# The routing of a mixture-of-experts layer with x turned unscaled, gathered parts made on VectorE by halves, and two sigmoids

## The reference

```
h = h + hgrn2_mixer(...)                      # the residual before
t = rms_norm_2(h, moe_norm).reshape(256, D)   # h * rsqrt(mean(h*h) + eps) * gain
logits = (t @ w_router).astype(F32)           # 256 x 8
top_vals, top_idx = lax.top_k(logits, 2)
top_w = jax.nn.softmax(top_vals, axis=-1)     # two weights per token
gates = jnp.sum(jax.nn.one_hot(top_idx, 8) * top_w[..., None], axis=1)
for e in range(8):
    out = out + gates[:, e:e + 1] * swiglu(t, w_gate[e], w_up[e], w_down[e])
```

## Time and profile before

| what | value |
|---|---|
| median of 3 runs | 1944.0 us (1942.25 to 1947.37) |
| the profiled execution, its own time | 1941.3 us |
| span of its records | 1939.4 us |
| busy in the span | PE 96%, DVE 80%, ACT 65%, POOL 1% |
| mean granted clock of TensorE | 0.981 of 2.4 GHz |

### The profile page before, as it was taken

The page is one execution under the profiler, slowest core; times in us unless marked ns, Lnnn a source line. Parts: engine busy times, 40 slices in busy tenths (PEclk is TensorE's granted clock), DMA queues, the critical chain, the costliest instruction groups (busy, mean ns, idle before and its releaser), DMA issues.

```text
span 1939.4 us, 27547 instructions
## 1 busy us (share of the span) xinstructions
PE 1854.3 (96%) x10240; PEld 1580.6 (82%) x10240; DVE 1552.2 (80%) x1589; ACT 1255.3 (65%) x1290; POOL 11.3 (1%) x9
## 2 busy tenths in 40 slices
PE   7888999998899999998799999999999999999997
PEld 7777999877799988876688888888888888888886
DVE  8966788476567645665898998989989899899997
ACT  6966565356554435554577777777777777777775
POOL 0000000000000000001000000000000000000000
PEclk9999999999799999999899999999999999999999
DMA  9422455542145554332499998999989989899894
GB/s 366 146 88 91 170 180 190 192 153 92 64 159 189 176 193 152 131 130 98 172 368 356 343 376 335 373 361 344 381 325 367 381 336 371 337 367 380 327 368 194
DMA packets 68330, 490.85 MB, mean 253 GB/s; under 512 B 7713, under 2 KB 8097, under 8 KB 8993
## 3 DMA queue, kind: packets, MB, share of 16 engines
q1 hardware_dynamic: 67968, 488.52, 67.1%
q0 software_dynamic: 288, 1.31, 0.2%
HBM read 488.75 MB, written 1.05 MB: 253 GB/s over the span
## 4 chain that ended last, share of the span: by engine, by line
PE 87%; DVE 6%; ACT 5%; issue 2%; DMA 0%; SPq 0%; ACTq 0%; DVEq 0%
PE ps L421 26%; PE ps L423 20%; PE ps L430 20%; PE ps L432 6%; PE ps L425 6%; DVE wl L2087 1%; PE ps L441 1%; PE ps L1322 1%; ACT wh L1401 1%; PE ps L1234 1%; PE ps L1053 1%; PE ps L467 1%; PE ps L1090 1%; PE ps L826 1%; PE ps L827 1%
## 5 line engine op out<-in xcount | busy, mean ns | idle before, releaser
L2990 DVE TENSOR_TENSOR wl<-raw,wh 128x2048 fp32r<-128x2048 f32 x336 | 761.1, 2288 | 63.3 <-ACT wh L2011 59.8
L2011 ACT ACTIVATE wh<-raw 128x2048 fp32r<-128x2048 f32 x336 | 642.1, 1918 | 180.9 <-PE ps L430 180.8
L421 PE MATMUL ps<-wh,hTh 128*128 128x512 f32 (+2 forms) x1128 | 443.2, 394 | 7.1 <-DVE hTl L2375 1.7
L2087 DVE TENSOR_TENSOR wl<-raw,wh 128x2048 fp32r<-128x2048 f32 x125 | 286.0, 2290 | 128.5 <-ACT wh L1401 127.9
L423 PE MATMUL ps<-wh,hTh 128*128 128x512 f32 x896 | 349.3, 390 | 0.0
L1401 ACT ACTIVATE wh<-raw 128x2048 fp32r<-128x2048 f32 x125 | 238.6, 1913 | 140.9 <-PE ps L430 73.2
L430 PE MATMUL ps<-wl,hTh 128*128 128x512 f32 (+2 forms) x1128 | 301.1, 386 | 0.0
L423 PE MATMUL ps<-wh,hTl 128*128 128x512 f32 (+2 forms) x680 | 260.4, 385 | 0.0
L421 PEld LDWEIGHTS ps<-wh,hTh 128*128 128x128 f32 x1128 | 212.2, 188 | 50.1 <-issue 5.4
L430 PEld LDWEIGHTS ps<-wl,hTh 128*128 128x128 f32 x1128 | 210.1, 188 | 42.8
L421 PE MATMUL ps<-hTh,wh 128*128 128x256 f32 x896 | 223.2, 286 | 2.5 <-DVE hTl L2127 2.3
(11 more groups left out here) (433 smaller groups left out, 2026.4 us busy)
## 6 DMA issues: line engine op xcount, KB each, us to landing
raw<-in_units SPq DMA_DIRECT2D x461, 1024.0 KB, 6.9
x<-in_x SPq DMA_DIRECT2D x2, 512.0 KB, 5.4
work<-in_lru_w SPq DMA_DIRECT2D x1, 1024.0 KB, 15.4
xn<-in_mem SPq DMA_DIRECT2D x1, 1024.0 KB, 17.5
out<-x SPq DMA_DIRECT2D x2, 512.0 KB, 3.4
consts<-in_consts POOLq DMA_DIRECT2D x1, 768.0 KB, 4.6
work<-in_moe_gain POOLq DMA_DIRECT2D x1, 512.0 KB, 3.8
consts<-in_consts SPq DMA_DIRECT2D x1, 352.0 KB, 11.5
```

Source lines behind the costliest of these rows:

```text
L421: nc.tensor.matmul(out, sh, mh, start=(first and j == 0), stop=False)
L2011: A(wh[:, n % SPLIT, :], raw[:, n % RAW, :], ACT.Copy).then_inc(sem("hi_made"), 1)
L2087: V.tensor_tensor(wl[:, n % SPLIT, :], raw[:, n % RAW, :], wh[:, n % SPLIT, :].bitcast(F32), ALU.subtract).then_inc(sem("lo_made"), 1)
L2990: V.tensor_tensor(wl[:, n % SPLIT, :], raw[:, n % RAW, :], wh[:, n % SPLIT, :].bitcast(F32), ALU.subtract).then_inc(sem("lo_made"), 1)
```

## The change

- `moe_norm_2` joins `SCALED_LATER`: TensorE turns x unscaled, into banks 4 to 7. The squares of token tile 0 are summed before ScalarE's `norm_high`, those of tile 1 behind it.
- The router's three products stand together for each k. The token's 1/std (`token_scale`) is applied when VectorE copies the turned logits to `L`.
- GpSimd computes nothing here. VectorE makes `tokens` from x, `token_scale` and the gain with `tokens_half`, and both differences with `tokens_rest`; everything about `parts` goes by halves of columns (512 of 1024, both token tiles). The first half of the gather waits for 4 steps, the second for 6 (`TOKEN_STEPS`).
- The gain is loaded into `xn` once the recurrent layer's output has been turned, not into `work` after the residual.
- The two weights are sigmoid(v1-v2) and sigmoid(v2-v1), both on ScalarE, in place of an exponential on ScalarE and three small operations on VectorE.
- VectorE makes the low part of expert unit 1 between the first and the second add of the residual, and that of unit 2, with the four memsets, behind `tokens_low`.

```diff
-    moe_gain = area(4096, D)
+    moe_gain = xn[:, 0, :]
...
+    TOKEN_STEPS = (4, 6)
...
-    NORM_BANK = {n: 4 if n in ("hgrn_norm_2", "ffn_norm_2") else 0 for n in NORMS}
-    SCALED_LATER = ("mem_attn_norm", "attn_norm_2", "ffn_norm_2")
+    NORM_BANK = {n: 4 if n in ("hgrn_norm_2", "ffn_norm_2", "moe_norm_2") else 0 for n in NORMS}
+    SCALED_LATER = ("mem_attn_norm", "attn_norm_2", "ffn_norm_2", "moe_norm_2")
...
@@ TensorE
-        split_product(ps[0:NE, 7, 0:S], [(rh[:, k * NE:(k + 1) * NE], rl[:, k * NE:(k + 1) * NE], hTh[:, k, :], hTl[:, k, :])
-                                         for k in range(KD)], ready=tile_ready, rest=lambda: None).then_inc(sem("logits"), 1)
+        for k in range(KD):
+            w = slice(k * NE, (k + 1) * NE)
+            tile_ready(k)
+            nc.tensor.matmul(ps[0:NE, 0, 0:S], rh[:, w], hTh[:, k, :], start=(k == 0), stop=False)
+            nc.tensor.matmul(ps[0:NE, 0, 0:S], rl[:, w], hTh[:, k, :], start=False, stop=False)
+            ins = nc.tensor.matmul(ps[0:NE, 0, 0:S], rh[:, w], hTl[:, k, :], start=False, stop=(k == KD - 1))
+        ins.then_inc(sem("logits"), 1)
...
-                pe.wait_ge(sem("tokens_left"), 3)
+                pe.wait_ge(sem("tokens_left"), TOKEN_STEPS[q])
...
@@ ScalarE
-        norm("moe_norm_2", N_FIXED + SPLIT)
-        for i in range(2):
-            act.wait_ge(sem("tokens_left"), i + 1)
-            A(parts[i][:], tokens[:], ACT.Copy).then_inc(sem("tokens_part"), 1)
+        A(warm, ones[:, 0:1], ACT.Sqrt)
+        norm_stats("moe_norm_2", (0,), False)
+        norm_high("moe_norm_2", 0)
+        norm_stats("moe_norm_2", (1,))
+
+        def token_part(i, h, left):
+
+            act.wait_ge(sem("tokens_left"), left)
+            cs = slice(h * HALF, (h + 1) * HALF)
+            A(parts[i][:, :, cs], tokens[:, :, cs], ACT.Copy).then_inc(sem("tokens_part"), 1)
+
+        token_part(0, 0, 1)
+        hi_to(N_FIXED + SPLIT)
+        token_part(1, 0, 2)
+        token_part(0, 1, 3)
+        token_part(1, 1, 5)
+        act.wait_ge(*reached("route_diff", 1))
+        A(rtv["w1"], rtv["v2"], ACT.Sigmoid, scale=-1.0)
+        A(rtv["w2"], rtv["v2"], ACT.Sigmoid).then_inc(sem("route_exp"), 1)
...
-        act.wait_ge(*reached("route_diff", 1))
-        A(rtv["ex"], rtv["v2"], ACT.Exp).then_inc(sem("route_exp"), 1)
...
@@ GpSimd
-        pool.wait_ge(*reached("x_ready", X_AFTER["hgrn"]))
+        pool.wait_ge(*reached("hgrn_oT_ps", 4))
         pool.dma_start(moe_gain, moe_gain_d.partition_broadcast(P)).then_inc(sem("moe_gain"), 16)
-        pool.wait_ge(*reached("norm_xn", TT * len(NORMS)))
-        pool.wait_ge(sem("moe_gain"), 16)
-        for t in range(TT):
-            ins = G_.tensor_tensor(tokens[:, t, :], xn[:, t, :], moe_gain, ALU.mult)
-        ins.then_inc(sem("tokens_left"), 1)
-        pool.wait_ge(sem("tokens_part"), 1)
-        pool.wait_ge(sem("tokens_left"), 1)
-        G_.tensor_tensor(tokens[:], tokens[:], parts[0][:], ALU.subtract).then_inc(sem("tokens_left"), 1)
...
@@ VectorE
-        residual("hgrn_x_change", 7, N_FIXED, 0)
+        residual("hgrn_x_change", 7, N_FIXED, 0, N_FIXED + 2)
...
-        norm("moe_norm_2", N_FIXED + SPLIT - 1)
+        norm_low("moe_norm_2", 0)
+        norm_rows("moe_norm_2")
+        token_scale = rstd[:, 2 * NORM_OF["moe_norm_2"]:2 * NORM_OF["moe_norm_2"] + TT]
...
+        def tokens_half(t, h):
+            cs = slice(h * HALF, (h + 1) * HALF)
+            return V.scalar_tensor_tensor(out=tokens[:, t, cs], in0=x[:, t, cs], scalar=token_scale[:, t:t + 1], in1=moe_gain[:, cs],
+                                          op0=ALU.mult, op1=ALU.mult)
+
+        def tokens_rest(i, h, part):
+
+            dve.wait_ge(sem("tokens_part"), part)
+            cs = slice(h * HALF, (h + 1) * HALF)
+            V.tensor_tensor((tokens, parts[2])[i][:, :, cs], tokens[:, :, cs], parts[i][:, :, cs],
+                            ALU.subtract).then_inc(sem("tokens_left"), 1)
...
-        V.tensor_copy(logitsT, ps[0:NE, 7, 0:S]).then_inc(sem("logits_read"), 1)
+        V.tensor_copy(logitsT, ps[0:NE, 0, 0:S]).then_inc(sem("logits_read"), 1)
+        tokens_half(0, 0)
+        tokens_half(1, 0).then_inc(sem("tokens_left"), 1)
...
-        lo_to(N_FIXED + SPLIT)
+        tokens_rest(0, 0, 1)
+        tokens_half(0, 1)
+        tokens_half(1, 1).then_inc(sem("tokens_left"), 1)
```

More of the change, by code:

```diff
@@ L314, in rows_of @@
     def rows_of(name):
-        return area(0, TT, D) if name == "mem_attn_norm" else xn
+        return {"mem_attn_norm": area(0, TT, D), "moe_norm_2": area(10240, TT, D)}.get(name, xn)
     def attention_heads(stage):
@@ L388, in build @@
     xsel = rcmp[1][:, 0:TT * NE].rearrange("p (t e) -> p t e", t=TT)
-    rtv = {k: tiny(2) for k in ("v1", "v2", "ex", "w1", "w2")}
+    rtv = {k: tiny(2) for k in ("v1", "v2", "w1", "w2")}
     posf = tiny(2)
@@ L1206, in _ @@
         pe.wait_ge(sem("router_lo"), 1)
[L1207 to L1208 removed]
+        for k in range(KD):
[5 more added lines that the diff above has]
+        ins.then_inc(sem("logits"), 1)
         pe.wait_ge(sem("logits_read"), 1)
         for t in range(TT):
[L1211 removed]
+            ins = nc.tensor.transpose(ps[:, 1, t * NE:(t + 1) * NE], logitsT[:, t * P:(t + 1) * P], ident[0:NE, 0:NE])
         ins.then_inc(sem("logits"), 1)
@@ L2141, in norm, with residual @@
             norm_low(name, ahead)
-        def residual(stage, n, following, bank=4):
+        def residual(stage, n, following, bank=4, then=0):
             lo_to(following + 1)
@@ L2147, in residual @@
                 for h in range(2):
+                    if 2 * t + h == 1:
+                        lo_to(then)
                     dve.wait_ge(*reached(stage, n - 3 + 2 * t + h))
@@ L2950, in _ @@
         choose(0)
-        dve.wait_ge(sem("tokens_part"), 2)
-        V.tensor_tensor(parts[2][:], tokens[:], parts[1][:], ALU.subtract).then_inc(sem("tokens_left"), 1)
-        dve.wait_ge(sem("tokens_left"), 3)
-        V.memset(GT.bitcast(F32), 0.0)
-        V.memset(gates[:, 0, :], 0.0)
-        V.memset(yh.bitcast(F32), 0.0).then_inc(sem("y_lo"), 1)
-        V.memset(yl.bitcast(F32), 0.0).then_inc(sem("y_lo"), 1)
-        def tokens_low(q, e):
-            dve.wait_ge(sem("tokens_hi"), e * 2 + q + 1)
-            V.tensor_tensor(xel[:, 4 * q:4 * q + 4, :], ps[:, TOKEN_BANKS[q], :].rearrange("p (a b) -> p a b", a=4),
-                            xeh[:, 4 * q:4 * q + 4, :].bitcast(F32), ALU.subtract).then_inc(sem("bank7_free"), 1)
+        tokens_rest(1, 0, 2)
+        tokens_rest(0, 1, 3)
         s1 = xsel
@@ L2971, in _, with tokens_low @@
         V.tensor_tensor(rtv["v2"], rtv["v2"], rtv["v1"], ALU.subtract).then_inc(sem("route_diff"), 1)
+        tokens_rest(1, 1, 4)
+        def tokens_low(q, e):
+            dve.wait_ge(sem("tokens_hi"), e * 2 + q + 1)
+            V.tensor_tensor(xel[:, 4 * q:4 * q + 4, :], ps[:, TOKEN_BANKS[q], :].rearrange("p (a b) -> p a b", a=4),
+                            xeh[:, 4 * q:4 * q + 4, :].bitcast(F32), ALU.subtract).then_inc(sem("bank7_free"), 1)
         for q in range(2):
             tokens_low(q, 0)
+        lo_to(N_FIXED + SPLIT)
+        V.memset(GT.bitcast(F32), 0.0)
+        V.memset(gates[:, 0, :], 0.0)
+        V.memset(yh.bitcast(F32), 0.0).then_inc(sem("y_lo"), 1)
+        V.memset(yl.bitcast(F32), 0.0).then_inc(sem("y_lo"), 1)
         dve.wait_ge(*reached("route_exp", 1))
-        step(V.tensor_scalar(rtv["w1"], rtv["ex"], 1.0, None, ALU.add))
-        step(V.reciprocal(rtv["w1"], rtv["w1"]))
-        step(V.tensor_tensor(rtv["w2"], rtv["w1"], rtv["ex"], ALU.mult))
         for t in range(TT):
```

7 lines of the change are left out of this document (5 added, 2 removed).

## The result

The changed kernel takes 1931.94 us (median of 15 runs, 1929.78 to 1940.71), the kernel before 1944.66 us beside it on the same chip (15 runs, 1941.49 to 1951.37). The ratio is 0.9938, with a 95% interval of 0.9926 to 0.9951: by it 12.1 us faster, between 9.5 and 14.4 (the two medians lie 12.7 apart). That is faster by more than 0.3% and inside the predicted range, but only 0.4 us from its low edge: the forecast was 1936, a gain of 7.9.

A forecast was written before the change was run, and what follows sets the result against it. TensorE bounds the experts, so only their start could move, behind 31.8 us of small steps. Experts 7.9 us earlier (between 7.4 and 8.4), all else nothing: 1944.0 - 7.9 = 1936 us, range 1931.5 to 1940.5.

The forecast's parts named there:

- the ceiling of the table loads: Experts' loop: TensorE idles 0.37 us per expert, so removing loads gives at most 8 x 0.37 = 3.0 us, 1933.1.
- the main case: Stretch ahead of the experts: they start 7.9 us earlier, median 1936 us; chance 0.66.
- Routing: From the recurrent layer's last product to the first expert product: experts start 7.4 or 8.4 us earlier, 7.9 taken.
- the upper bound of their price: Products of x, scale and gain: at most the whole 1.226 us each, 0.744 taken; bounds give a gain of 5.2 to 8.8.
- the 3.75 of GpSimd's end: Ranking, VectorE's product at L2922: without GpSimd's subtraction it takes 0.23 instead of 3.98 us, 3.75 less.
- Covers: Low parts, table load, sigmoids, zeros and gates lie beside other work and cost nothing; the thinnest has 0.6 us to spare.
- VectorE's backlog: Rival at the experts' start: some 6.4 us of moved VectorE work makes TensorE wait; time about 1950, chance 0.04.
- handovers: Rival in the chain of halves: eight ScalarE-VectorE handovers eat part, gain 3 to 5.5, 1938.5 to 1941; chance 0.10.
- The table loads in the loop: Rival in the experts: two loads per expert leave and were on TensorE's path, at most 3.0 us; chance 0.06.
- The loads' whole length, 20.5 us: Experts' loop: 16 x 1.283 us of ScalarE; if each load held up TensorE, the time would be 1915.6.
- Cold experts: Rival at the experts' start: first 4.6 us run at 1.2 GHz, losing 2.0; gain 5.4, 1938.6; chance 0.14.
- the offset of 2.7: Whole kernel: the runs' median lies 2.7 us above the profiled execution, added to turn 1933.4 into 1936.

The follow-up runs named there:

- loads_back: Changed kernel plus a one-element exponential on ScalarE ahead of the experts' loop, so both table loads stand in each expert again; 1938.42 us, ratio 0.9952.
- before_sigmoids: Kernel before with only the two sigmoids in place of the exponential and three small VectorE steps; 1939.69 us, ratio 0.997.
- unit_early: Changed kernel with the low part of expert unit 2 moved back to right behind the ranking; 1942.88 us in a single execution.
- turned_scaled: Changed kernel with x scaled before it is turned, tiles' squares summed ahead and the gain loaded late, as before the change; 1940.77 us, ratio 0.9976.
- after_again: The changed kernel once more, unchanged, as control on another chip; 1935.97 us, ratio 0.9938.
- reordered_busy: Changed kernel with unread TensorE products in its waits, VectorE's steps reordered for one gather, sigmoids behind the copies of gathered halves; 1931.24 us, ratio 0.9925.
- pool_writes: Changed kernel with three GpSimd memsets of 1024 columns beside the ranking, results unread; 1931.04 us in a single execution.

## Why the prediction was right, and where it was wrong

The routing came out as worked out, and it is most of the gain. That the median fell inside the range owes something to luck: the range's low end was put there for the ceiling of the table loads, a rival at 0.06, and that rival came true beside the main case, which the forecast had not added up. With 3.0 less of width there, the range would begin at 1934.5, and the measured 1931.94 would lie outside.

**Routing: right, to a few tenths.** In distances from the last product, predicted and measured: logits copied 6.20 and 6.28; the turned logits 7.95 and 7.95; behind the ranking 10.45 and 10.48; slots 13.05 and 12.94; first gather half 16.6 and 16.16 (the one-hot matrix waits 0.26 for its slots, where before it waited 0.61); second half 20.3 and 19.75; first expert product 24.4 at the low clock and 24.06, 23.4 with a rise and 22.84. The gain is 7.70 or 8.92, predicted 7.4 or 8.4. The two products of x, scale and gain took 1.39 and 1.41 a pair, predicted 1.41; the upper bound of their price is gone. The long one of the two products at L2957 (was L2922) took 3980 ns in the earlier trace rows; now the pair takes 0.48 us as drawn, 224 and 227 ns each, so the 3.75 of GpSimd's end is there in full.

**Covers: right.** The low part between the adds, the table load and the sigmoids (931.64 to 933.2, done as the second half begins to be gathered at 933.13; ScalarE's copy of the first half waits behind them, and nobody waits for it), the zeros and the gates cost nothing: where the experts start at the high clock, the first scatter stands 5.55 to 5.59 behind the start, as before, and the experts keep their distance. The rival by VectorE's backlog did not occur, and neither did that of the handovers.

**The step that failed: "The table loads in the loop" as a rival with 0.06, and nothing for them in the sum.** The prediction says of the experts "Nothing but fewer products or an earlier start helps there", read from 124.63 busy of 125 us. The small rival's own figure, 8 x 0.37 = 3.0, is almost what was measured, 2.7, shown in both directions by `loads_back` and `before_sigmoids`. I took an idle time of 0.37 us as too little to look into. It deserved two questions: which wait ends there, and what stands ahead of it; the load's 1.28 us, VectorE's wait of 0.94 and the backlog behind it were all in the trace of before. Nor was the 0.37 the ceiling that I called it: TensorE's idle time in an expert is 0.30 without the loads, 0.07 less for 0.36 gained, since a gap between pipelined products hides behind their drawn ends. That the total nearly met the ceiling is chance. The loads' whole length, 20.5 us, and the 42.6 estimated from the Trainium skill were far off, as weighed: only what outlasts the buffers between three engines arrives at TensorE.

**Cold experts: the mechanism was there, its size was low, and it is no property of the kernel alone.** It cost 8.38 - 5.57 = 2.8 where 2.0 was taken: I priced 4.6 us at the low clock and a loss of 40%, but it lasted almost 6, and a product came every 0.43 us instead of every 0.23, a loss of 47%. Two profiles of the changed kernel have it and one doesn't, with the same steps at the same distances. In `loads_back`, `unit_early` and `turned_scaled` the clock rose sooner, and it cost 1.4, 1.8 and 2.0.

**From the profile to the median: the offset of 2.7 was carried over, and that is not sound to the microsecond.** What stands ahead of the change can move the time by as much as the change itself. The window from 500 to 900, in before and in `loads_back`, over code which the change doesn't touch:

```profile
500.00:900.00 400.00, 388.16 (x2520) 340.63 (x2519) 244.48 (x316) 189.65 (x244) 0.00 (x0) 0.97 0.41 145
```

```profile
500.00:900.00 400.00, 388.66 (x2485) 341.46 (x2485) 238.66 (x313) 187.33 (x244) 0.00 (x0) 0.95 0.41 143
```

The rows have 2520 and 2485 matmuls in 400 us, at 0.97 and 0.95. The clock is not all of it: `after_again` has 0.97 in this window too, and its recurrent layer ends 5.80 us later than that of before. What else moves it stays open. In the eleven profiles with the changed norm and the same code ahead of it, the recurrent layer's end lies between 907.91 (`reordered_busy`) and 916.06 (`loads_back`). The two first profiles then add up: 1939.4 + 6.13 (a later end of that layer) - 7.70 (routing) + 2.81 (cold start) - 2.7 (experts) = 1937.9, against a span of 1938.1.

**The sum by the shortest executions.** If in these the clock rises in the second half and the experts start at the high clock, as in the profile of `pool_writes` (22.84 and 5.55), the gain is 8.9 + 2.7 = 11.6. The fastest run of before in all series was 1940.85, that of the changed kernel 1929.78: 11.1. With the low clock throughout the gather it is 7.7 + 2.7 = 10.4. The measured 12.1 (9.5 to 14.4) holds both; on the other two chips it was 12.1 (8.2 to 16.0) and 9.5 (6.0 to 13.0) by the same kernels. Whether the true gain lies nearer 10.4 or 11.6 can't be told from these. Against the forecast of 7.9, the table loads are 2.7 of what is more, the clock's rise and the routing's few tenths the rest as far as it can be placed.

## What to carry to other kernels

A small idle time of the engine that bounds a loop is worth following back once, engine by engine: here 0.06 us of it stood for 0.32, and behind it stood a table load that a single function ahead of the loop decides. An engine that is busy for 99.7% of a loop can still have a third of a percent to give. Take GpSimd's reads out of the stretch in which VectorE's small steps are the chain, and give TensorE something to turn as soon as its input exists, since a wait costs it the clock as well. And compare stages from their own start: two profiled executions of one kernel can differ by more than the change is worth.
